# Expert weights in 2 MB pieces with 16 KB runs, activations turned in 32x32 blocks on VectorE

## The chip, the cores and the metric

The kernel runs on one core of one Trainium2 chip. The metric is the device time of one execution in microseconds (us). "Before" was run three times.

## What is computed

One encoder layer over 512 tokens of width 1024, all in float32: three token mixers with gates, then a mixture of 32 experts of which each token takes 4. The mixers are not touched by this change. The experts are:

```python
logits = ht @ w_router + b_router
top_v, top_i = lax.top_k(logits, 4);  gate = softmax(top_v)
# tokens are sorted by expert and worked on in blocks
def expert_block(xb, e):
    gu = xb @ w_gate_up[e] + b_gate_up[e]            # 1024 -> 2048
    g = minimum(gu[:, :1024], 7.0)
    lin = clip(gu[:, 1024:], -7.0, 7.0)
    act = g * sigmoid(1.702 * g) * (lin + 1.0)
    return act @ w_down[e] + b_down[e]               # 1024 -> 1024
y = segment_sum(rows * gate)                         # back to the tokens
x = rmsnorm(x + y, norm_final)
```

## The kernel before, in words

The program is written engine by engine, with semaphores between them; nothing reorders it. Each engine runs its own list, and a wait holds up everything behind it on that engine.

The mixers and the router fill the first part. Then comes the expert loop. A **job** is one expert with up to 96 token rows ("slots"); with these inputs there are 32 jobs, numbered 0 to 31. Per job, TensorE runs `gate_up(j)` and `down(j)`, and it works one job ahead: `gate_up(0)`, then in the loop `gate_up(j + 1)`, `down(j)`, and at the end `down_last(31)`.

- `gate_up` has 8 **parts**, one for each 128 rows of the contraction. Each part uses 1 MB of weights (`gu_w`), and runs 12 matmuls of 128x32 by 128x512 (24 records in the trace, since a float32 matmul leaves two). Ahead of the parts stand three small matmuls that write the bias (`bias_row` times `bias_of`).
- `down` has 4 parts of 1 MB (`dn_w`) with 24 matmuls of 128x32 by 128x256 each (48 records).
- The 96 rows of a job are fetched by an indirect DMA of GpSimd (`xg`), turned by TensorE with eight transposes against the identity (`turn_tokens`, at line 1434, after the first part of `down`) and copied by ScalarE into `xt`.
- After `gate_up`, ScalarE and VectorE make the activation: `sigmoid`, `clamp`, `activate`, which writes `act_sb` at line 1323. TensorE turns it with six transposes (`turn_act`) after part 1 of the next `gate_up`, and VectorE copies the result out of PSUM into `act_t` (`take_act`, line 1311), which `down` uses.
- After `down`, VectorE multiplies by the gate into `y_sb` (line 1331), and GpSimd adds the rows to `x_rows` in DRAM by three indirect DMAs.

Weights are loaded by the queue of SyncE (SP), in the order of its list. `gu_w` has two sets of eight buffers, `dn_w` one set of four. In the loop SP waits until a part of TensorE is done (`wait_part`, on the semaphore `gemm_ps`) and then issues the load into the buffer that it freed. A piece of `gu_w` or `dn_w` is one DMA of 128 partitions with 8 KB each. In the list the eight loads for `gate_up(j + 3)` stand behind the last `dn` load of `down(j)`, so they are issued in one go at the end of `down(j)`.

In job 0, between two parts of `gate_up`, TensorE also makes the tables of slots (`slot_tables`); the loop's first fetches of rows, and SP's loads of the last two pieces for job 1, wait for them. At the end, SP loads `final_gain` and `down_bias`, which `down_last`'s accumulation needs first.

Of the kernel before, what the change touches and what calls it, by code (L numbers as in the profile page):

```python
# [10 lines left out]
F32 = mybir.dt.float32  # L11
# [97 lines left out]
def encoder_kernel(nc, x, mem, norm_mix, w_in, q_norm_a, k_norm_a, sink_b, norm_mem, w_mem_kv,  # L109
# [3 lines left out]
    with ctx:  # L113
# [149 lines left out]
        gu_w = [sb(f"gu_w{i}", [P, 2 * D], F32, at * KIB) for i, at in enumerate(GU_AT)]  # L263
        dn_w = [sb(f"dn_w{i}", [P, 2 * D], F32, at * KIB) for i, at in enumerate(DN_AT)]
# [72 lines left out]
        gu_in = [sem(f"gu_in{i}") for i in range(16)]  # L337
        dn_in = [sem(f"dn_in{i}") for i in range(4)]
# [100 lines left out]
        at_ps = sem("at_ps")  # L439
# [115 lines left out]
        def _(sp):  # L555
# [44 lines left out]
            def load_gu(e, s, k):  # L600
                sp.dma_start(gu_w[s * KD + k][:], wgu[e, :, k, :]).then_inc(gu_in[s * KD + k], 16)  # L601

            def load_dn(e, q):
                sp.dma_start(dn_w[q][:], wdn[e, q, :, :]).then_inc(dn_in[q], 16)
# [17 lines left out]
            for k in (6, 7):
                load_gu(0, 0, k)
            for q in (0, 1):
                load_dn(0, q)
# [8 lines left out]
            for q in (2, 3):  # L634
                load_dn(0, q)
# [1254 lines left out]
```

## Time and profile before

| what | value |
|---|---|
| median of 3 runs | 1553.23 us (1552.82 to 1557.38) |
| the profiled execution | 1558.09 us, span 1556.2 us |
| TensorE (PE) busy | 1515.6 us, 97% |
| VectorE (DVE), ScalarE (ACT), GpSimd (POOL) busy | 27%, 19%, 15% |
| HBM read | 457.94 MB, 307 GB/s over the span |
| the weight loads | 256 of `gu_w` and 128 of `dn_w`, 1 MB each |

How to read the rows below. In a **timeline**, a row is the start in the span, the length, engine and line, the operation with "output <- input" and shape, the number of instructions merged into the row, and in brackets how long the engine had been idle before and what ended that. PE is the matmul side of TensorE; SPq and POOL issue DMAs. In a row of **windows**: stretch, its length, the busy time of PE, PEld (weight loads), DVE, ACT and POOL (number of instructions), granted clock of TensorE (1.00 is 2.4 GHz, 0.50 is 1.2 GHz), the mean share of the 16 DMA engines, GB/s. In rows of **DMA issues**: count, size of one, median us from issue to landing. [...]

### The profile page before, as it was taken

To read this page: it belongs to the slowest core of one execution; us is meant where nothing else is said; L and a number is where in the kernel's file an instruction comes from. 1 tells how busy PE (TensorE), PEld (TensorE's weight loads), DVE (VectorE), ACT (ScalarE), POOL (GpSimd) and SP (SyncE) were. 2 spreads that over 40 slices of the span, in tenths; PEclk is the share of its full clock that TensorE was granted. 3 is DMA by queue.
4 is the path that set the end of the run, shared out by engine and by line. 5 is a ranking of instruction groups with operands and counts; after the bars stand their busy time and mean duration, and the time that the engine had idled before them with its cause. 6 is when DMAs were issued, how large, how long until landed. Compare 5 with 4: busy or idle time off the path is not lost.

```text
span 1556.2 us, 35152 instructions
## 1 busy us (share of the span) xinstructions
PE 1515.6 (97%) x15156; PEld 780.8 (50%) x15156; DVE 423.5 (27%) x642; ACT 291.0 (19%) x519; POOL 225.8 (15%) x321
## 2 busy tenths in 40 slices
PE   8999999999989999999999999999999999999987
PEld 7866688888843343344333344433344443334432
DVE  3758722525532111121111121111121111112112
ACT  5468822323201000010000010000010000010001
POOL 0000030000010221111221111221111221111120
PEclk9999999999989999999999999999999999999998
DMA  7310022334768999999999999999999999999963
GB/s 266 120 67 22 8 91 75 123 140 186 289 254 299 388 387 384 396 387 401 396 387 390 387 398 395 391 388 386 386 395 393 385 379 383 384 384 395 407 226 126
DMA packets 98139, 468.75 MB, mean 301 GB/s; under 512 B 18360, under 2 KB 26832, under 8 KB 48912
## 3 DMA queue, kind: packets, MB, share of 16 engines
q1 hardware_dynamic: 79712, 450.35, 74.0%
q0 software_dynamic: 18048, 17.71, 5.6%
q8 instruction: 31, 0.51, 0.1%
q10 hardware_dynamic: 336, 0.08, 0.0%
q14 instruction: 12, 0.10, 0.0%
HBM read 457.94 MB, written 19.79 MB: 307 GB/s over the span
## 4 chain that ended last, share of the span: by engine, by line
PE 91%; DVE 3%; DMA 3%; SPq 1%; issue 1%; ACT 0%; ACTq 0%; DVEq 0%
PE ps L1755 41%; PE ps L1770 20%; PE ps L1407 6%; PE ps L1409 6%; PE ps L1408 6%; PE ps L1434 5%; DMA gu_w<-in_w_gate_up 2%; PE ps L1785 1%; PE ps L1560 1%; SPq L601 1%; DVE head_max L1086 1%; PE ps L1747 1%; PE ps L1516 1%; DVE probs L1104 1%; PE ps L1678 1%
## 5 line engine op out<-in xcount | busy, mean ns | idle before, releaser
L1755 PE MATMUL ps<-gu_w,xt 128*32 128x512 f32 x6144 | 675.6, 595 | 0.7 <-DMA gu_w<-in_w_gate_up 0.7
L1755 PEld LDWEIGHTS ps<-gu_w,xt 128*32 128x32 f32 x6144 | 192.9, 110 | 438.7 <-issue 434.3
L1770 PE MATMUL ps<-dn_w,act_t 128*32 128x256 f32 x5952 | 333.4, 380 | 0.1
L1770 PEld LDWEIGHTS ps<-dn_w,act_t 128*32 128x32 f32 x5952 | 189.7, 110 | 140.8 <-issue 15.4
L864 ACT ACTIVATE sg_sb<-ps,limits 128x768 f32<-128x768 f32 x32 | 28.9, 902 | 902.4 <-PE ps L1755 902.4
L1315 DVE TENSOR_SCALAR lin_sb<-ps 128x768 f32<-128x768 f32 x32 | 30.7, 958 | 493.0 <-ACT sg_sb L864 493.0
L949 POOL DMA_INDIRECT x_rows<-y_sb,sum_row x93 | 144.8, 1557 | 37.3 <-issue 37.3
L933 POOL TENSOR_TENSOR mark_sb<-ones 1x1 f32<-1x1 f32 x93 | 29.7, 319 | 796.9 <-DVE y_sb L1331 780.8
L1407 PE MATMUL ps<-w_high,h_hi 128*128 128x512 f32 x352 | 138.2, 392 | 0.6 <-DVE mem_lo L1032 0.5
L1409 PE MATMUL ps<-w_high,h_lo 128*128 128x512 f32 x352 | 137.1, 389 | 0.0
L1408 PE MATMUL ps<-w_low,h_hi 128*128 128x512 f32 x352 | 137.0, 389 | 0.0
L512 DVE TENSOR_TENSOR w_low<-w_raw,w_high 128x2048 fp32r<-128x2048 f32 (+2 forms) x36 | 63.9, 1813 | 116.1 <-ACT w_high L504 116.1
L1331 DVE TENSOR_TENSOR y_sb<-ps,y_gate 128x768 f32<-128x768 f32 x31 | 29.7, 957 | 206.6 <-PE ps L1770 206.6
L1311 DVE COPY act_t<-ps 128x768 f32<-128x768 f32 x32 | 30.6, 958 | 174.6 <-PE ps L1434 167.9
L1407 PEld LDWEIGHTS ps<-w_high,h_hi 128*128 128x128 f32 x352 | 66.1, 188 | 15.0 <-DVE mem_lo L1032 0.8
L1409 PEld LDWEIGHTS ps<-w_high,h_lo 128*128 128x128 f32 x352 | 66.1, 188 | 13.8
L1408 PEld LDWEIGHTS ps<-w_low,h_hi 128*128 128x128 f32 x352 | 66.1, 188 | 13.2
L504 ACT ACTIVATE w_high<-w_raw 128x2048 fp32r<-128x2048 f32 (+2 forms) x36 | 53.5, 1537 | 19.5 <-PE ps L1409 17.6
L1323 DVE SCALAR_TENSOR_TENSOR act_sb<-lin_sb,sg_sb 128x768 f32<-128x768 f32 x32 | 50.7, 1584 | 3.3
L756 ACT ACTIVATE probs<-ps,neg_max 128x512 f32<-128x512 f32 (+2 forms) x64 | 37.5, 595 | 5.5 <-DVE neg_max L1089 5.2
L943 POOL DMA_INDIRECT xg<-h_rows,gather_row x32 | 33.0, 1033 | 26.1 <-issue 20.0
L860 ACT ACTIVATE xt<-ps 128x768 f32<-128x768 f32 x32 | 25.9, 811 | 56.5 <-PE ps L1434 56.5
(255 smaller groups left out, 1006.0 us busy)
## 6 DMA issues: line engine op xcount, KB each, us to landing
gu_w<-in_w_gate_up SPq DMA_DIRECT2D x256, 1024.0 KB, 25.3
dn_w<-in_w_down SPq DMA_DIRECT2D x128, 1024.0 KB, 18.7
w_raw<-in_w_in SPq DMA_DIRECT2D x8, 2048.0 KB, 7.9
w_raw<-in_w_out SPq DMA_DIRECT2D x2, 2048.0 KB, 7.7
w_raw<-in_w_in SPq DMA_DIRECT2D x2, 1024.0 KB, 7.5
x_sb<-in_x SPq DMA_DIRECT2D x8, 256.0 KB, 7.0
w_raw<-in_w_mem_kv SPq DMA_DIRECT2D x1, 2048.0 KB, 10.1
x<-in_x SPq DMA_DIRECT2D x4, 512.0 KB, 5.0
```

Source lines behind the costliest of these rows:

```text
L504: nc.scalar.activation(wh[u % 2][:, a * COLS:b * COLS], raw[u % 2][:, a * COLS:b * COLS], ACT.Copy).then_inc(wh_done, 1)
L512: nc.vector.tensor_tensor(wl[u % 2][:, a * COLS:b * COLS], raw[u % 2][:, a * COLS:b * COLS], wh[u % 2][:, a * COLS:b * COLS].bitcast(F32), ...
L756: nc.scalar.activation(probs[:, 2 * (s % 2) + g, 0:w], ps[:, 2 * (s % 2) + g, 0:w], ACT.Exp, bias=neg_max[:, s % 2, g:g + 1], scale=SCALE, ...
L943: nc.gpsimd.indirect_dma_start(out=xg[s][:], out_offset=None, in_=h2_rows, in_offset=bass.IndirectOffsetOnAxis(ap=rows, axis=0), bounds_ch ...
L949: nc.gpsimd.indirect_dma_start(out=x_rows.rearrange("r (q n) -> (r q) n", q=4), out_offset=bass.IndirectOffsetOnAxis(ap=sum_row[:, s, g:g ...
L1323: nc.vector.scalar_tensor_tensor(out=act_sb[:].rearrange("p (h g) c -> p (g c) h", h=2), in0=lin_sb[:].rearrange("p g (c h) -> p (g c) h", ...
L1407: nc.tensor.matmul(bank, hi, w_hi, start=start, stop=False)
L1408: nc.tensor.matmul(bank, hi, w_lo, start=False, stop=False)
L1409: return nc.tensor.matmul(bank, lo, w_hi, start=False, stop=stop)
L1434: return nc.tensor.transpose(ps[0:src.shape[1], bank, col:col + n], src, ident[0:n, 0:n])
L1755: last = nc.tensor.matmul(ps[quarter(q), g, :], xt[:, k, quarter(g)], w[:].rearrange("p (h n) -> p h n", h=2)[:, :, q * QCOLS:(q + 1) * QC ...
L1770: last = nc.tensor.matmul(ps[quarter(q), 3 + g, 0:QCOLS], act_t[:, TRIOS * h + g, quarter(c)], dn_w[c][:, h * D + q * QCOLS:h * D + (q + 1 ...
```

## The change

1. The weights are laid out differently. `gate_up`'s contraction row on partition p of part c is now row 8p + c, in place of 128c + p, and likewise for `down`. One DMA loads two parts: 128 partitions with 16 KB of consecutive rows each, 2 MB. Semaphores and SP's waits go by pairs.
2. To match, `turn_tokens` picks every eighth column of `xg`, and `activate` writes `act_sb` in blocks of 32 columns.
3. The six transposes of TensorE for the activation are gone, and the copy out of PSUM with them. VectorE does one `transpose` (32x32 blocks, SBUF to SBUF) in `turn_act`, after `take_y`. ScalarE waits for `act_ready` before it overwrites `sg_sb`.
4. `bias_of` is loaded and cast at the program's start, by ScalarE's queue and GpSimd, in place of SP and VectorE ahead of the expert loop.
5. `slot_tables` run after part 2 of `gate_up(0)`, in place of part 4.
6. `final_gain` and `down_bias` are loaded ahead of the last `dn` loads.

```diff
-        gu_w = [sb(f"gu_w{i}", [P, 2 * D], F32, at * KIB) for i, at in enumerate(GU_AT)]
-        dn_w = [sb(f"dn_w{i}", [P, 2 * D], F32, at * KIB) for i, at in enumerate(DN_AT)]
+        gu_pair = [sb(f"gu_pair{i}", [P, 4 * D], F32, at * KIB) for i, at in enumerate(GU_AT[0::2])]
+        dn_pair = [sb(f"dn_pair{i}", [P, 4 * D], F32, at * KIB) for i, at in enumerate(DN_AT[0::2])]
+        gu_w = [gu_pair[i // 2][:, (i % 2) * 2 * D:(i % 2 + 1) * 2 * D] for i in range(16)]
+        dn_w = [dn_pair[i // 2][:, (i % 2) * 2 * D:(i % 2 + 1) * 2 * D] for i in range(4)]
...
-        wgu = w_gate_up[0].rearrange("e (k p) n -> e p k n", p=P)
-        wdn = w_down[0].rearrange("e (q p h) n -> e q p (h n)", p=P, h=2)
+        wgu = w_gate_up[0].rearrange("e (p k a) n -> e k p (a n)", p=P, a=2)
+        wdn = w_down[0].rearrange("e (p q h) n -> e q p (h n)", p=P, h=4)
...
             sp.wait_ge(gate_t_ps, 1)
-            for k in range(KD - 2, KD):
-                load_gu(e_one, 1, k)
+            load_gu(e_one, 1, GU_PAIRS - 1)
...
-                    for k in range(KD):
-                        wait_part(sp, i, b * PARTS + k)
-                        if k == 0:
+                    for m in range(GU_PAIRS):
+                        wait_part(sp, i, b * PARTS + 2 * m + 1)
+                        if m == 0:
                             load_bias(e_gu, b)
-                        load_gu(e_gu, b, k)
-                    for q in range(DN_PARTS):
-                        wait_part(sp, i, stream(b, KD + q))
-                        load_dn(e_dn, q)
+                        load_gu(e_gu, b, m)
+                    for m in range(DN_PAIRS):
+                        wait_part(sp, i, stream(b, KD + 2 * m + 1))
+                        load_dn(e_dn, m)
             e_last = sp.value_load(job_table[0:1, 0, bass.ds(pairs_but_one * 2 + 1, 1)], min_val=0, max_val=N_EXP - 1)
-            for q in range(DN_PARTS):
-                wait_part(sp, pairs_but_one, stream(0, KD + q))
-                load_dn(e_last, q)
-
-
             wait_part(sp, pairs_but_one, stream(0, KD - 1))
             sp.dma_start(final_gain[:], norm_final.rearrange("(a n) -> a n", a=1).to_broadcast([P, D])).then_inc(fgain_in, 16)
             for t in range(TB):
                 sp.dma_start(down_bias[N_EXP * t:N_EXP * (t + 1), :], b_down[0]).then_inc(down_bias_in, 16)
+            for m in range(DN_PAIRS):
+                wait_part(sp, pairs_but_one, stream(0, KD + 2 * m + 1))
+                load_dn(e_last, m)
...
+            act.dma_start(bias_of_raw[:], fixed[:, 5 * P + 8:6 * P + 8]).then_inc(bias_of_in, 16)
...
+                    act.wait_ge(act_ready, j + 1)
                     sigmoid(j + 1)
...
+            pool.wait_ge(bias_of_in, 16)
+            nc.gpsimd.tensor_copy(bias_of[:], bias_of_raw[:]).then_inc(bias_of_ready, 1)
...
-            def take_act(j):
-                dve.wait_ge(at_ps, j + 1)
-                nc.vector.tensor_copy(act_t[:].rearrange("p (a k) m -> p a (k m)", a=2), ps[:, 6:8, 0:TRIOS * P]).then_inc(act_t_done, 1)
+            def turn_act(j):
+                dve.wait_ge(act_ready, j + 1)
+                nc.vector.transpose(act_t[:], act_sb[:]).then_inc(act_t_done, 1)
...
-                nc.vector.scalar_tensor_tensor(out=act_sb[:].rearrange("p (h g) c -> p (g c) h", h=2), in0=lin_sb[:].rearrange("p g (c h) -> p (g c) h", h=2),
-                                               scalar=1.0, in1=sg_sb[:].rearrange("p g (c h) -> p (g c) h", h=2),
+                nc.vector.scalar_tensor_tensor(out=act_sb[:].rearrange("p (c x) -> p x c", c=KD), in0=lin_sb[:].rearrange("p g (i c) -> p (g i) c", c=KD),
+                                               scalar=1.0, in1=sg_sb[:].rearrange("p g (i c) -> p (g i) c", c=KD),
...
-            dve.wait_ge(bias_of_in, 16)
-            nc.vector.tensor_copy(bias_of[:], bias_of_raw[:]).then_inc(bias_of_ready, 1)
...
-                    take_act(j)
                     wait_part(dve, i, stream(b, KD - 1))
                     clamp(j + 1)
+                    dve.wait_ge(act_t_done, j + 1)
                     activate(j + 1)
                     wait_part(dve, i, stream(b, PARTS - 1))
                     take_y(j, b)
-            take_act(pairs_but_one * 2)
+                    turn_act(j + 1)
...
             wait_part(dve, pairs_but_one, stream(0, PARTS - 1))
-            take_act(pairs_but_one * 2 + 1)
+            turn_act(pairs_but_one * 2 + 1)
             take_y(pairs_but_one * 2, 0)
...
-                if k == 4:
+                if k == 2:
                     pe.wait_ge(vals_ready, 1)
...
             def turn_tokens(s):
                 for k in range(KD):
-                    last = turn(6 + k // 4, (k % 4) * SLOTS, xg[s][:, k * P:(k + 1) * P])
+                    last = turn(6 + k // 4, (k % 4) * SLOTS, xg[s][:].rearrange("s (p k) -> s k p", k=KD)[:, k, :])
                 last.then_inc(x_ps, 1)
-
-            def turn_act(j):
-                pe.wait_ge(act_ready, j + 1)
-                for k in range(2 * TRIOS):
-                    last = turn(6 + k // TRIOS, (k % TRIOS) * P, act_sb[:, k, :])
...
+
+            def act_part(k, g):
+
+                return act_t[:, k * SLOTS + QUARTER * g:k * SLOTS + QUARTER * (g + 1)]
...
                 for k in range(KD):
                     w = gu_w[s * KD + k]
-                    pe.wait_ge(gu_in[s * KD + k], loads * 16)
+                    if k % 2 == 0:
+                        pe.wait_ge(gu_in[s * GU_PAIRS + k // 2], loads * 16)
...
                 for c in range(DN_PARTS):
-                    pe.wait_ge(dn_in[c], j * 16 + 16)
+                    if c % 2 == 0:
+                        pe.wait_ge(dn_in[c // 2], j * 16 + 16)
                     for h in range(2):
                         for g in range(TRIOS):
                             for q in range(4):
-                                last = nc.tensor.matmul(ps[quarter(q), 3 + g, 0:QCOLS], act_t[:, TRIOS * h + g, quarter(c)],
+                                last = nc.tensor.matmul(ps[quarter(q), 3 + g, 0:QCOLS], act_part(2 * c + h, g),
...
             pe.wait_ge(gs_ready, j + 1)
             pe.wait_ge(l_ready, j + 1)
-            gate_up(j + 1, 1, pairs_but_one + 1, last_act_but_one)
-            down(j, last_act_of_all)
+            gate_up(j + 1, 1, pairs_but_one + 1, lambda k: None)
+            down(j, lambda q: None)
```

How the lists change, at three places. On TensorE, in the loop, around the second part of `gate_up` (each buffer of before serves one part, each pair of after two). Before:

```order
L1755 MATMUL ps<-gu_w_158,xt 32x512 x11
L1755 MATMUL ps<-gu_w_159,xt 32x512 [waits gu_in1]
L1755 MATMUL ps<-gu_w_159,xt 32x512 x11
L1434 MATMUL ps<-ident,act_sb 128x128 [waits act_ready]
L1434 MATMUL ps<-ident,act_sb 128x128 x5
L1755 MATMUL ps<-gu_w_160,xt 32x512 [waits gu_in2]
```

And now:

```order
L1753 MATMUL ps<-gu_pair_158,xt 32x512 [waits gu_in0]
L1753 MATMUL ps<-gu_pair_158,xt 32x512 x23
L1753 MATMUL ps<-gu_pair_159,xt 32x512 [waits gu_in1]
L1753 MATMUL ps<-gu_pair_159,xt 32x512 x23
L1753 MATMUL ps<-gu_pair_160,xt 32x512 [waits gu_in2]
```

The turns of `act_sb` are gone, and only every other part waits for a load. On VectorE, one job of the loop (`under_limit`, `sg_ready` come from ScalarE, `gemm_ps` from TensorE, `added` from GpSimd's scatter). Before:

```order
L1311 COPY act_t<-ps 128x768 [waits at_ps]
L550 ISA
L1314 REGISTER_ALU [waits gemm_ps]
L1315 TENSOR_SCALAR lin_sb<-ps 128x768 [waits under_limit]
L1319 SCALAR_TENSOR_TENSOR sg_sb<-ps,sg_sb 128x768 [waits sg_ready]
L1323 SCALAR_TENSOR_TENSOR act_sb<-lin_sb,sg_sb 128x384x2 [waits gs_ready,l_ready]
L550 REGISTER_ALU
L1330 ISA [waits gate_kept,gemm_ps]
L1331 TENSOR_TENSOR y_sb<-ps,y_gate 128x768 [waits added]
```

And now:

```order
L1313 ISA [waits gemm_ps]
L1314 TENSOR_SCALAR lin_sb<-ps 128x768 [waits under_limit]
L1350 REGISTER_ALU
L1318 SCALAR_TENSOR_TENSOR sg_sb<-ps,sg_sb 128x768 [waits sg_ready,act_t_done]
L1322 SCALAR_TENSOR_TENSOR act_sb<-lin_sb,sg_sb 128x96x8 [waits gs_ready,l_ready]
L553 REGISTER_ALU
L1329 ISA [waits gate_kept,gemm_ps]
L1330 TENSOR_TENSOR y_sb<-ps,y_gate 128x768 [waits added]
L1310 STREAM_TRANSPOSE act_t<-act_sb 128x768 [waits act_ready]
```

The copy at the job's start is replaced by a transpose at its end, behind `y_sb`. On SP, after the loop, the loads for the last job. Before:

```order
L604 ISA [waits gemm_ps]
L604 DMA dn_w_176<-in_w_down 128x2048
L550 REGISTER_ALU
L604 ISA [waits gemm_ps]
L604 DMA dn_w_177<-in_w_down 128x2048
L550 REGISTER_ALU
L666 DMA final_gain<-in_norm_final 128x1024 [waits gemm_ps]
L668 DMA down_bias<-in_b_down 32x1024 x4
```

And now:

```order
L553 ISA
L657 DMA final_gain<-in_norm_final 128x1024 [waits gemm_ps]
L659 DMA down_bias<-in_b_down 32x1024 x4
L553 REGISTER_ALU
L607 ISA [waits gemm_ps]
L607 DMA dn_pair_166<-in_w_down 128x4096
L553 REGISTER_ALU
L607 ISA [waits gemm_ps]
L607 DMA dn_pair_167<-in_w_down 128x4096
```

`final_gain` and the four loads of `down_bias` stand ahead of the two `dn` loads, which wait for two parts each.

## Rows read from the trace of the kernel before

**Rows 1.** The head of the profile's page.
```profile
span 1556.2 us, 35152 instructions
```

**Rows 2.** Windows: the loop, the start of the experts, and `down_last`.
```profile
900.00:1000.00 100.00, 100.00 (x1205) 40.95 (x1199) 15.99 (x16) 8.02 (x11) 19.48 (x27) 1.00 1.02 391
...
441.00:446.00 5.00, 5.00 (x27) 1.19 (x28) 0.00 (x0) 0.00 (x0) 1.05 (x1) 0.50 1.02 433
...
1524.00:1528.00 4.00, 4.00 (x17) 0.96 (x18) 0.00 (x0) 0.00 (x0) 0.00 (x0) 0.50 1.01 401
```

**Rows 3.** Timeline of TensorE over one job of the loop.
```profile
1007.54 5.36 PE L1755 MATMUL ps<-gu_w,xt 128*32 128x512 f32 x48
1012.83 0.87 PE L1434 MATMUL ps<-ident,act_sb 128*128 128x128 f32 x6
1013.63 15.66 PE L1755 MATMUL ps<-gu_w,xt 128*32 128x512 f32 x144
...
1031.81 0.88 PE L1434 MATMUL ps<-ident,xg 96*128 96x96 f32 x8
```

**Rows 4.** Timeline of VectorE: `y_sb` of two neighbouring jobs, and of two four apart.
```profile
1241.28 0.96 DVE L1331 TENSOR_TENSOR y_sb<-ps,y_gate 128x768 f32<-128x768 f32 x1 [6.85 <-PE ps L1770]
...
1274.70 0.96 DVE L1331 TENSOR_TENSOR y_sb<-ps,y_gate 128x768 f32<-128x768 f32 x1 [6.86 <-PE ps L1770]
...
1308.24 0.96 DVE L1331 TENSOR_TENSOR y_sb<-ps,y_gate 128x768 f32<-128x768 f32 x1 [6.99 <-PE ps L1770]
...
1444.10 0.96 DVE L1331 TENSOR_TENSOR y_sb<-ps,y_gate 128x768 f32<-128x768 f32 x1 [7.09 <-PE ps L1770]
```

**Rows 5.** DMA issues of `dn_w`, from 500 to 600 and from 1300 to 1400.
```profile
dn_w<-in_w_down SPq DMA_DIRECT2D x12, 1024.0 KB, 7.2
...
dn_w<-in_w_down SPq DMA_DIRECT2D x12, 1024.0 KB, 29.9
```

**Rows 6.** The page's groups: VectorE's copy out of PSUM and its strided product.
```profile
L1311 DVE COPY act_t<-ps 128x768 f32<-128x768 f32 x32 | 30.6, 958 | 174.6 <-PE ps L1434 167.9
...
L1323 DVE SCALAR_TENSOR_TENSOR act_sb<-lin_sb,sg_sb 128x768 f32<-128x768 f32 x32 | 50.7, 1584 | 3.3
```

**Rows 7.** Timeline from the first job to the first `dn` load of the loop.
```profile
440.38 1.66 POOL L972 TENSOR_TENSOR job_vals<-job_hots,dest_vals 128x880 f32<-128x880 f32 x1
...
440.49 0.80 PE L1747 MATMUL ps<-bias_row,bias_of 8*128 8x512 f32 x3 [5.80 <-issue]
441.22 15.65 PE L1755 MATMUL ps<-gu_w,xt 128*32 128x512 f32 x120
...
472.38 0.51 PE L1747 MATMUL ps<-bias_row,bias_of 8*128 8x512 f32 x3 [1.04 <-DVE sg_sb L1319]
...
497.36 6.46 SPq L604 DMA_DIRECT2D dn_w<-in_w_down  x3
```

**Rows 8.** DMA, 10 to 17 (2 KB packets) and 437 to 450 (8 KB).
```profile
DMA packets 1422, 2.75 MB, mean 393 GB/s; under 512 B 80, under 2 KB 80, under 8 KB 1422
...
q1 hardware_dynamic: 1422, 2.75, 105.3%
...
DMA packets 716, 5.27 MB, mean 405 GB/s; under 512 B 73, under 2 KB 73, under 8 KB 73
...
q1 hardware_dynamic: 716, 5.27, 97.1%
```

**Rows 9.** Timeline of the end: last part of `down(30)` to `down_last`'s result.
```profile
1507.98 2.80 PE L1770 MATMUL ps<-dn_w,act_t 128*32 128x256 f32 x48
...
1520.45 3.78 PE L1837 MATMUL ps<-down_bias,gate_t 32*128 32x512 f32 x8 [9.67 <-DMA down_bias<-in_b_down]
...
1524.16 16.05 PE L1785 MATMUL ps<-dn_w,act_t 128*32 128x512 f32 x96
1540.28 1.26 ACT L895 ACTIVATE y_hi_last<-ps,last_gate 96x512 fp32r<-96x512 f32 x2 [37.26 <-PE ps L1785]
```

More of the change, by code:

```diff
@@ L271, in encoder_kernel @@
         xg = [sb(f"xg{i}", [SLOTS, D], F32, (166 + 4 * i) * KIB) for i in range(2)]
-        act_t = sb("act_t", [P, 2 * TRIOS, P], F32, 174 * KIB)
+        act_t = sb("act_t", [P, KD * SLOTS], F32, 174 * KIB)
         lin_sb = sb("lin_sb", [P, TRIOS, QCOLS], F32, 177 * KIB)
         sg_sb = sb("sg_sb", [P, TRIOS, QCOLS], F32, 180 * KIB)
-        act_sb = sb("act_sb", [P, 2 * TRIOS, P], F32, 184 * KIB)
+        act_sb = sb("act_sb", [P, KD * SLOTS], F32, 184 * KIB)
         same_slot = sb("same_slot", [SLOTS, TRIOS, P], F32, 196 * KIB)
@@ L336, in encoder_kernel @@
         first_in = sem("first_in")
-        gu_in = [sem(f"gu_in{i}") for i in range(16)]
-        dn_in = [sem(f"dn_in{i}") for i in range(4)]
+        gu_in = [sem(f"gu_in{i}") for i in range(8)]
+        dn_in = [sem(f"dn_in{i}") for i in range(2)]
         bias_of_in = sem("bias_of_in")
@@ L598, in _, with load_gu, load_dn @@
                 sp.dma_start(x2[:, t, :], x[0, t * P:(t + 1) * P, :]).then_inc(x2_in, 16)
[L600 to L604, printed above, removed]
+            def load_gu(e, s, m):
+                sp.dma_start(gu_pair[s * GU_PAIRS + m][:], wgu[e, m, :, :]).then_inc(gu_in[s * GU_PAIRS + m], 16)
+            def load_dn(e, m):
+                sp.dma_start(dn_pair[m][:], wdn[e, m, :, :]).then_inc(dn_in[m], 16)
             def load_bias(e, s):
@@ L610, in _ @@
             sp.wait_ge(bias_stored, 256)
-            sp.dma_start(bias_of_raw[:], fixed[:, 5 * P + 8:6 * P + 8]).then_inc(bias_of_in, 16)
             load_bias(0, 0)
-            for k in (0, 1):
-                load_gu(0, 0, k)
+            load_gu(0, 0, 0)
             for n in range(2):
                 sp.wait_ge(wl_done, 2 * (UNITS - 1 + n))
-                for k in (2 + 2 * n, 3 + 2 * n):
-                    load_gu(0, 0, k)
+                load_gu(0, 0, 1 + n)
             sp.dma_start(h2_rows[SEQ:SEQ + SLOTS, :], x[0, 0:SLOTS, :]).then_inc(rows_out, 16)
             sp.wait_ge(gemm_ps, GEMMS[UNITS - 1])
[L622 to L625, printed above, removed]
+            load_gu(0, 0, 3)
+            load_dn(0, 0)
             for t in range(TB):
@@ L633, in _ @@
             sp.wait_ge(gemm_ps, G1)
-            for q in (2, 3):
-                load_dn(0, q)
+            load_dn(0, 1)
             sp.wait_ge(table_ready, 1)
@@ L639, in _ @@
             load_bias(e_one, 1)
-            for k in range(KD - 2):
-                load_gu(e_one, 1, k)
+            for m in range(GU_PAIRS - 1):
+                load_gu(e_one, 1, m)
             sp.wait_ge(vals_ready, 1)
             sp.wait_ge(gate_t_ps, 1)
-            for k in range(KD - 2, KD):
-                load_gu(e_one, 1, k)
+            load_gu(e_one, 1, GU_PAIRS - 1)
             pairs_but_one = sp.value_load(job_table[0:1, 1, 1:2], min_val=MIN_PAIRS - 1, max_val=NJ // 2 - 1)
@@ L888, in _ @@
             wait_part(act, pairs_but_one, stream(0, KD - 1))
+            act.wait_ge(act_ready, pairs_but_one * 2 + 1)
             sigmoid(pairs_but_one * 2 + 1)
@@ L1344, in _ @@
             activate(0)
+            turn_act(0)
             take_sum_rows()
@@ L1720, in turn_tokens @@
                 for k in range(KD):
-                    last = turn(6 + k // 4, (k % 4) * SLOTS, xg[s][:, k * P:(k + 1) * P])
+                    last = turn(6 + k // 4, (k % 4) * SLOTS, xg[s][:].rearrange("s (p k) -> s k p", k=KD)[:, k, :])
                 last.then_inc(x_ps, 1)
-            def turn_act(j):
-                pe.wait_ge(act_ready, j + 1)
-                for k in range(2 * TRIOS):
-                    last = turn(6 + k // TRIOS, (k % TRIOS) * P, act_sb[:, k, :])
-                last.then_inc(at_ps, 1)
             def spread_slots():
@@ L1780, in down_last @@
                 for c in range(DN_PARTS):
-                    pe.wait_ge(dn_in[c], j * 16 + 16)
+                    if c % 2 == 0:
+                        pe.wait_ge(dn_in[c // 2], j * 16 + 16)
                     for h in range(2):
@@ L1784, in down_last @@
                             for g in range(TRIOS):
-                                last = nc.tensor.matmul(ps[quarter(g), 4 + n, :], act_t[:, TRIOS * h + g, quarter(c)],
+                                last = nc.tensor.matmul(ps[quarter(g), 4 + n, :], act_part(2 * c + h, g),
                                                         dn_w[c][:, h * D + n * COLS:h * D + (n + 1) * COLS],
@@ L1813, in _ @@
                     pe.wait_ge(l_ready, j + 1)
-                    gate_up(j + 1, 1 - b, i + 1 + b, last_act)
+                    gate_up(j + 1, 1 - b, i + 1 + b, lambda k: None)
                     if b == 0:
```

17 lines of the change are left out of this document (5 added, 12 removed).

## Prediction

> Times are span microseconds unless said otherwise. The profiled execution took 1558.1 us, its span is 1556.2 [rows 1], and the median of the runs shown is 1553.2. I work in the span and carry the difference over to the median.
>
> **What bounds the kernel now.** I read the windows first. In the expert loop TensorE is busy without a gap at full clock, and the DMA engines show a share of 1.02 beside it [rows 2]. So two things are full at once, and the question is which one sets the pace. The timeline of TensorE gives what a job consists of: gate_up, in its middle the six turns of act_sb, then down with eight turns of xg after its first part [rows 3]. The 144 records after the act turns take 15.66 us and the 48 before them 5.36, so a record costs 10.30/96 = 0.107 us. 48 of them end 5.15 us after 1007.54, at 1012.69, and the next gate_up record starts at 1013.63: the act turns cost the path **0.94 us** a job.
>
> The starts of y_sb, one a job, are 33.42 us apart (1241.28 to 1274.70), and four jobs later on average 33.97 (135.86/4) [rows 4]. The times to landing say why: a piece of dn_w landed 7.2 us after its issue around 550 and 29.9 around 1350 [rows 5]. A piece is issued when its buffer is read and needed one job, 33.4 us, later. The queue was slower than TensorE all along; it ate the slack and at about 1300 TensorE began to wait a little. So: **PE pace 33.42, queue's own pace 33.97** (12 pieces of 1 MB a job), and the kernel ends as the slack is gone. A change that only frees TensorE meets the queue. That is the core of the case.
>
> **The change, part by part.**
>
> *Act turns leave TensorE.* 33.42 - 0.94 = 32.48 a job. VectorE does a 32x32 block transpose of 128x768 instead of the copy out of PSUM. The trace has no such operation: the nearest rows are the copy, 958 ns, and the strided product, 1584 ns [rows 6]; I take 1.3 us. In the loop it runs after y_sb and is wanted a whole gate_up later, over 20 us, so it costs nothing there. Without that cover it would cost its 1.3 us; it has none once, in front of down_last. The product's new write pattern (eight elements in place of two inside) and ScalarE's new wait on act_ready, met a job earlier, are hidden in down too.
>
> *The start.* TensorE stood 5.80 us in front of its first bias matmul at 440.49, whose operand bias_of VectorE casts late. GpSimd does that at the program's start now, so gate_up(0) can start once xt is there, near 435.7 in place of 441.22: 5.5 us. Its first 120 records took 15.65 us [rows 7], partly at the lower of the two clock levels, 1.2 GHz (0.50 granted, 441 to 446, after that idle time [rows 2]); at 0.107 us they take 12.9. That is 2.8 more. The slot tables move from part 4 to part 2: reached at 435.7 + 7.7 = 443.4, while GpSimd's last product for them ended at 442.04 [rows 7], so no wait, but with 1.4 us to spare only. gate_up(1) begins at 472.38 - 8.3 = **464.1**. The tables' turn also releases the fourth pair of gu(1) some 13 us earlier, so the queue doesn't run dry at 455; it still does ahead of down(0).
>
> *Pairs of 2 MB.* dn(1) is what the queue waits for at the start: issued at 497.36, 24.98 after gate_up(1) began [rows 7]. Now it needs two parts of down(0) and the xg turns (2.6 + 0.9) but no act turns (0.9): 464.1 + 27.5 = **491.6**. After that the queue is never empty. A pair needs both its parts free and both landed, up to 5 us less slack out of 26; once the queue sets the pace this costs only the time of the last pair's two parts, 5.2 us.
>
> *16 KB runs.* Price per packet by two stretches [rows 8]: 1342 packets of 2 KB (without 80 small ones) in 105.3% of 7 us x 16 engines, at most 88 ns each; 643 of 8 KB (without 73) in 97.1% of 13 x 16, 314 ns. Four of 2 KB cost 351, so each packet has some 12 ns of its own; two of 8 KB joined save 12 of 628, 1.9%. Of 33.97 that is at most 0.6; the scatter and gather share the queue and keep theirs. I take 0.47: **pace 33.5**. Bounds: 33.97 (nothing saved) above, and below 33.2, under which TensorE is the limit again. The rows are now 64 KB apart (dn: 32 KB) in place of end to end. The 2 KB packets of w_raw came from rows 18 KB apart and lost nothing but their own 12 ns, so I put no price on that; the other side is a rival. The Trainium skill (DMA: Bandwidth & Descriptors, Latency and other measured facts) reports falling rates with row pitch from 2 MiB up and the full rate at 512 KiB. By that rule nothing is lost here; this trace has no such pitch.
>
> *Strided xg.* The eight turns of xg now load every eighth element. Their time is unchanged in my sum; see the rivals.
>
> *The end.* Down(30) ends at 1507.98 + 2.80 = 1510.8. Then TensorE stood 9.67 us for down_bias, issued behind the last dn piece, ran the bias matmuls for 3.78 us and down_last for 16.05, its first 4 us at granted clock 0.50 [rows 2, 9]. Now final_gain and down_bias are issued at the end of gate_up(31), 11 us ahead. Counted from the end of down(30): transpose 1.3, y_sb 1.0 = 2.3; bias matmuls 2.0 at full clock; down_last 13.9; the rest as before, 1556.2 - 1540.28 = 15.9. Sum **34.1** for 45.4. What is late next: dn(31)'s pairs. In queue order they land some 3.4 and 9.1 us after down(30)'s end (1 MB of gains and biases, then 2 MB at 5.7 each); down_last wants them at 4.3 and 11. It fits, closely.
>
> **The sum.** Two chains; the later one ends down(30).
> - TensorE: 464.1 + 31 x 32.48 = 1471.0, less 0.9, since down(30) has no turns left at all: 1470.1. (The same for before: 472.38 + 31 x 33.42 = 1508.4, and 2.4 of waits, 1510.8.)
> - Queue: dn(1) to dn(30) and gu(3) to gu(31), 352 MB or 29.33 jobs: 491.6 + 29.33 x 33.5 = 1474.2, and 5.2 for the last two parts: **1479.4**. (Before: 497.4 + 29.33 x 33.97 = 1493.7.)
>
> 1479.4 + 34.1 = 1513.5, that is 42.7 less than 1556.2; median 1553.2 - 42.7 = **1510.5**, said as 1511. 11.3 of it come from the end, 31.4 from what lies before (8.3 of these from TensorE's start). The queue takes back some 8 us of what TensorE could have had.
>
> **Rivals.**
> 1. *Nothing saved by longer runs.* Pace 33.97: queue 1488.0, down(30) 1493.2, median 1524. For it: the 12 ns come from different stretches. Chance 0.14.
> 2. *TensorE remains the limit.* Pace under 33.2: 1470.1 + 34.1, median 1501. It can't be beaten without a TensorE gain that I see nowhere. 0.13.
> 3. *Strided xg is dear.* No row loads weights with a stride. A turn of xg spaces out at 0.88/8 = 0.11 us [rows 3]; if each doubled, the job is back to nearly 33.4, down(30) ends at 464.1 + 31 x 33.4 = 1499.5, median 1531. Against it: the loads run beside the matmuls. The Trainium skill (SBUF — State Buffer, Door 1) says that an access needs two hits in a 16-byte line for full rate; a 32-byte step has one. By that rule this rival holds; no row shows it. 0.10.
> 4. *Slower, the other side: scattered runs.* If reads 64 KB apart slow the queue, median = 1510.5 + 29.33 x (pace - 33.5). From a pace of 34.96, 2.9% over today's, the kernel is slower than before; at 5% over, 35.7, it is 1575. For it: all the loop's bytes come so, and nothing else can absorb it. Against: the 18 KB rows. 0.10.
> 5. *The end keeps a wait* (dn(31) late): up to 11 back, 1522. 0.05.
>
> My forecast, pace 33.2 to 33.9, has 0.48 and by itself spans 1501 to 1522.
>
> **Numbers.** About 0.3% (5 us) is what a measurement of this kernel tells from no change. The range must hold the forecast, rivals 1, 2, 3 and 5: 1500 to 1533. Faster 0.88 (all but rival 4 and some sum of misfortunes), same 0.03, slower 0.09.
>
> **What would show it.** Right: y_sb starts 32.5 us apart at first and about 33.5 later; waits of TensorE on dn_pair and gu_pair, growing from the middle on; 16 KB packets near 616 ns, one engine's time; no idle of 5.8 at 435 and none of 9.7 after down(30); clock 1.00 at both places. Wrong: 33.4 from the first job on with no DMA wait (rival 3), a pace over 34 with full queue (rival 4), a stall at the slot tables, or down_last waiting for dn_in.

## Result, and the profile after

The changed kernel takes 1540.7 us (median of four, 1538.3 to 1542.1), the kernel before beside it 1555.3 (four, 1552.8 to 1557.8). The ratio is 0.9904, 95% interval 0.9879 to 0.9929: faster by 1%, where I had forecast nearly 3%; the measured time lies outside my range. The profiled execution took 1541.8 us. Of the run e14 below, two of six executions took 2567 and 2967 us and are left out of its time; what disturbed them is not known.

First VectorE's timeline after the change: `y_sb` of the first two jobs, and of two jobs thirteen apart (compare [rows 4]).

```profile
499.89 0.96 DVE L1330 TENSOR_TENSOR y_sb<-ps,y_gate 128x768 f32<-128x768 f32 x1 [6.99 <-PE ps L1769]
532.62 0.96 DVE L1330 TENSOR_TENSOR y_sb<-ps,y_gate 128x768 f32<-128x768 f32 x1 [7.07 <-PE ps L1769]
...
990.88 0.96 DVE L1330 TENSOR_TENSOR y_sb<-ps,y_gate 128x768 f32<-128x768 f32 x1 [7.14 <-PE ps L1769]
...
1439.44 0.96 DVE L1330 TENSOR_TENSOR y_sb<-ps,y_gate 128x768 f32<-128x768 f32 x1 [9.00 <-PE ps L1769]
```

A job takes 32.73 us at first, and does so for fifteen jobs. From 990.88 on it takes (1439.44 - 990.88)/13 = 34.50 us. That is slower than any job of the kernel before. Windows say the same: span 1539.9, and between 1300 and 1400 TensorE is no longer full (columns as in [rows 2]; why a DMA share can pass 1.00, as in [rows 8] for one queue alone, no run here shows).

```profile
900.00:1000.00 100.00, 99.79 (x1205) 40.67 (x1201) 15.94 (x15) 8.22 (x12) 20.37 (x31) 1.00 1.02 394
1300.00:1400.00 100.00, 96.05 (x1121) 37.16 (x1117) 16.07 (x15) 8.22 (x12) 19.50 (x27) 1.00 1.01 384
```

The waits of TensorE over the whole span (us in total, times, longest): the late jobs wait for the second matrix.

```profile
PE ps L1769 <- DMA dn_pair<-in_w_down: 15.2, 25, 1.3
...
PE ps L1744 <- DVE sg_sb L1318: 2.6, 1, 2.6
...
PE ps L1753 <- DMA gu_pair<-in_w_gate_up: 0.6, 3, 0.2
```

The loads between 500 and 600, then between 1300 and 1400 (compare [rows 5]):

```profile
gu_pair<-in_w_gate_up SPq DMA_DIRECT2D x12, 2048.0 KB, 20.1
dn_pair<-in_w_down SPq DMA_DIRECT2D x7, 2048.0 KB, 9.9
...
gu_pair<-in_w_gate_up SPq DMA_DIRECT2D x12, 2048.0 KB, 37.5
dn_pair<-in_w_down SPq DMA_DIRECT2D x6, 2048.0 KB, 28.3
```

The start (compare [rows 7]) and the end ([rows 9]):

```profile
464.26 0.80 PE L1744 MATMUL ps<-bias_row,bias_of 8*128 8x512 f32 x3 [2.60 <-DVE sg_sb L1318]
464.98 23.19 PE L1753 MATMUL ps<-gu_pair,xt 128*32 128x512 f32 x192
...
494.75 5.51 SPq L607 DMA_DIRECT2D dn_pair<-in_w_down  x2
...
1503.95 0.98 DVE L1310 STREAM_TRANSPOSE act_t<-act_sb 128x768 f32<-128x768 f32 x1 [5.80 <-PE ps L1769]
1504.85 0.92 DVE L1330 TENSOR_TENSOR y_sb<-ps,y_gate 128x768 f32<-128x768 f32 x1
1505.92 2.28 PE L1825 MATMUL ps<-down_bias,gate_t 32*128 32x512 f32 x8 [2.04 <-DVE y_sb L1330]
...
1508.13 15.29 PE L1785 MATMUL ps<-dn_pair,act_t 128*32 128x512 f32 x96
```

gate_up(1) starts at 464.26. The wait of 9.67 us ahead of down_bias is gone. Down(30) ends at 1503.9: 6.9 us earlier than before, where I had expected 31.4.

**A view of my own.** The semaphore of a load is raised 16 times, and the trace has the times. The page counts 16 DMA engines, and I read each signal as that of one engine; the trace does not name them. For one `dn` load, in us after the first of the 16:

```
kernel, issued at   the sixteen engines in order of landing
before,  1301.0     0 .1 .1 .1 .1 .2 .7 .7 1.1 1.3 1.4 3.5 5.6 10.9 14.5 21.7
after,    560.2     0 .2 .3 .9 1.0 1.2 1.4 1.4 1.6 1.7 1.7 2.0 2.2 2.3 2.5 2.5
after,    920.2     0 .1 .1 .8 1.5 2.9 6.1 7.1 8.6 8.7 11.3 11.9 12.4 13.8 15.9 16.3
after,   1301.0     0 .3 .4 .4 .4 .8 1.0 1.1 1.7 2.6 7.9 11.0 11.4 15.0 17.8 22.0
```

So "the queue" is not one thing. In both kernels some engines fall behind, job by job, until the last is about 22 us late, while ten or eleven of the sixteen land within 3 us of each other at 1301. TensorE may start only after the last of the 16 signals. The landing time of [rows 5] is that of the laggards. Below, "lag" is the last number of such a row.

### The profile page after: what moved, and what is told of

It is laid out like the page before. It is cut to its first block, busy times and chain, and to the rows that moved or that the text cites. A ratio compares the mean times of both kernels' runs of the same rounds, so it can differ in the third digit from the quotient of the medians.

```text
span 1539.9 us, 34114 instructions
## 1 busy us (share of the span) xinstructions
PE 1496.6 (97%) x14964; PEld 768.7 (50%) x14964; DVE 420.0 (27%) x641; ACT 290.9 (19%) x519; POOL 226.3 (15%) x322
## 3 DMA queue, kind: packets, MB, share of 16 engines
q0 software_dynamic: 18048, 17.71, 5.5%
## 4 chain that ended last, share of the span: by engine, by line
PE 71%; DMA 25%; DVE 3%; ACT 1%; issue 0%; ACTq 0%; SPq 0%; DVEq 0%
PE ps L1753 26%; DMA dn_pair<-in_w_down 24%; PE ps L1769 17%; PE ps L1406 6%; PE ps L1408 6%; PE ps L1407 6%; PE ps L1433 3%; PE ps L1785 1%; PE ps L1559 1%; DVE head_max L1085 1%; PE ps L1515 1%; DVE probs L1103 1%; PE ps L1677 1%; PE ps L1744 1%; PE ps L1442 0%
## 5 line engine op out<-in xcount | busy, mean ns | idle before, releaser
L1753 PE MATMUL ps<-gu_pair,xt 128*32 128x512 f32 x6144 | 670.2, 595 | 1.2 <-DMA gu_pair<-in_w_gate_up 0.6
L1753 PEld LDWEIGHTS ps<-gu_pair,xt 128*32 128x32 f32 x6144 | 195.3, 110 | 454.4 <-issue 431.1
L1769 PE MATMUL ps<-dn_pair,act_t 128*32 128x256 f32 x5952 | 336.2, 380 | 15.3 <-DMA dn_pair<-in_w_down 15.2
L1769 PEld LDWEIGHTS ps<-dn_pair,act_t 128*32 128x32 f32 x5952 | 187.6, 110 | 162.3 <-DMA dn_pair<-in_w_down 34.9
L1407 PEld LDWEIGHTS ps<-w_low,h_hi 128*128 128x128 f32 x352 | 66.1, 188 | 13.3
L505 ACT ACTIVATE w_high<-w_raw 128x2048 fp32r<-128x2048 f32 (+2 forms) x36 | 53.5, 1538 | 19.5 <-PE ps L1408 17.6
L1433 PEld LDWEIGHTS ps<-ident,xg 96*128 96x128 f32 x256 | 30.9, 204 | 13.2 <-issue 12.3
```

What stands on the lines that cost most here:

```text
L505: nc.scalar.activation(wh[u % 2][:, a * COLS:b * COLS], raw[u % 2][:, a * COLS:b * COLS], ACT.Copy).then_inc(wh_done, 1)
L1407: nc.tensor.matmul(bank, hi, w_lo, start=False, stop=False)
L1433: return nc.tensor.transpose(ps[0:src.shape[1], bank, col:col + n], src, ident[0:n, 0:n])
L1753: last = nc.tensor.matmul(ps[quarter(q), g, :], xt[:, k, quarter(g)], w.rearrange("p (h n) -> p h n", h=2)[:, :, q * QCOLS:(q + 1) * QCOLS ...
L1769: last = nc.tensor.matmul(ps[quarter(q), 3 + g, 0:QCOLS], act_part(2 * c + h, g), dn_w[c][:, h * D + q * QCOLS:h * D + (q + 1) * QCOLS], s ...
```

## Experiments

The question was why some engines lag. The page counts GpSimd's gathers and scatters (queue q0 below) on the same 16 engines. Their rows are valid only up to the count of an expert's tokens (40 to 96 of 96 slots, 64 on average) and the rest is skipped. Places are filled from slot 0 up, so the work lies on the first partitions.

**e1, slots spread.** Where a place's slot is chosen, the two comparisons get another order of the same numbers:

```diff
-tensor_tensor(slot_hot[:], counter[:, 0:SLOTS].rearrange("p (a j) -> p a j", a=1) ...
+tensor_tensor(slot_hot[:].rearrange("p c (x b) -> p c x b", b=4),
+              counter[:, 0:SLOTS].rearrange("p (a b x) -> p a x b", a=1, b=4) ...
```

> The changed kernel, with consecutive places of an expert's tokens put on slots four apart (slot 4x+b holds place 24b+x), so that the rows which gathers and scatters really move lie on all partitions and not on the first ones of each block; the output stays the reference's. Theory 1 (the slowest DMA engines set the pace, and they are slow because the scatter and gather rows fall on few engines): the spread between the first and the last engine's landing of a load falls from about 20 us to under 8 us, TensorE's jobs in the second half take 33.0 to 33.3 us and not 34.5, and the time is 1518 to 1527 us. Theory 2 (the engines lag for another reason: long runs, or a fixed difference of the engines): spread and pace stay, 1538 to 1543 us.

Measured: **1518.9 us**, ratio 0.9767 (0.9754 to 0.9781). Every job takes 32.73 us:

```profile
501.14 0.96 DVE L1332 TENSOR_TENSOR y_sb<-ps,y_gate 128x768 f32<-128x768 f32 x1 [6.99 <-PE ps L1771]
...
1417.49 0.96 DVE L1332 TENSOR_TENSOR y_sb<-ps,y_gate 128x768 f32<-128x768 f32 x1 [7.00 <-PE ps L1771]
```

That is 916.35/28 = 32.73. Packets and bytes are the same in both kernels. Queue q0 is that of the gathers and scatters, over the whole span (packets, MB, share of 16 engines):

```profile
q1 hardware_dynamic: 51920, 450.27, 74.4%
q0 software_dynamic: 18048, 17.71, 5.5%
```

Only the place of the rows differs. The lag is 6.9 at 921 us and 13.3 at 1314, and stays under 16; in the changed kernel TensorE's waits came at about 20. Theory 1 holds in its cause and its time. Two of its sizes were off: the lag is not under 8, and the late jobs take 32.73 us, not 33.0 to 33.3.

**e2, the start and the end alone.** The kernel before, with:

```diff
-            sp.dma_start(bias_of_raw[:], ...)       # on SP, cast by VectorE late
+            act.dma_start(bias_of_raw[:], ...)      # on ACT, cast by GpSimd early
-                if k == 4:                          # slot_tables
+                if k == 2:
-            for q in range(DN_PARTS): ... load_dn(e_last, q)
             sp.dma_start(final_gain[:], ...)
             for t in range(TB): sp.dma_start(down_bias[...], ...)
+            for q in range(DN_PARTS): ... load_dn(e_last, q)
```

> The kernel before with only what the change did outside the loop: bias_of made early, the slot tables at block 2 of gate_up(0), the last down loads behind the final gain and bias. The loop (1 MB pieces, turns on TensorE) stays. Theory 1 (in the loop both kernels go at the pace of the slowest DMA engines, so the change of the loop bought next to nothing; start 3 to 6 us and end 9 to 10 us are the whole gain): 1539 to 1543 us, as the changed kernel. Theory 2 (the loop change gave about half): 1546 to 1551 us.

Measured: **1540.2 us**, 0.9905 (0.9888 to 0.9922), the changed kernel's time. The whole change of the loop bought nothing that I can measure here.

**e3, loads of 1 MB,** the changed kernel with runs of 8 KB:

```diff
-wgu = w_gate_up[0].rearrange("e (p k a) n -> e k p (a n)", p=P, a=2)
+wgu = w_gate_up[0].rearrange("e (p k) n -> e k p n", p=P)
-wdn = w_down[0].rearrange("e (p q h) n -> e q p (h n)", p=P, h=4)
+wdn = w_down[0].rearrange("e (p q h) n -> e q p (h n)", p=P, h=2)
```

> The changed kernel with loads of 1 MB and runs of 8 KB (rows 8p+c and the block transposes stay). Theory 1 (the length of a run does not matter where the slowest engine sets the pace): 1538 to 1543 us. Theory 2 (16 KB runs save 0.47 us a job as I summed it): 29 jobs by 0.47 is 14 us more, 1550 to 1556 us. Theory 3 (2 MB pieces come free later, two blocks at once, and that costs the queue its lead): less, 1525 to 1535 us.

Measured: **1539.9 us**, 0.9898 (0.9883 to 0.9913). Run length and piece size changed together, and their sum does not show in the time. It shows in the lag: 17.7 us at 827 us in e3, 12.5 in the changed kernel, at the same 32.73 us a job. So long runs may have helped the late engines, and the larger pieces may have taken it back; no run here parts the two.

**e4, e3 with the old rows,** its turns of xg unstrided:

```diff
-wgu = ... "e (p k) n -> e k p n"            wdn = ... "e (p q h) n -> e q p (h n)"
+wgu = ... "e (k p) n -> e k p n"            wdn = ... "e (q p h) n -> e q p (h n)"
-xg[s][:].rearrange("s (p k) -> s k p", k=KD)[:, k, :]
+xg[s][:, k * P:(k + 1) * P]
```

> The 1 MB kernel of the run above, and the weights' rows taken as before (128 neighbouring rows of w_gate_up a piece, 256 of w_down, each piece one stretch of memory), with the unstrided turns of xg; the rows of w_down then do not match the order of the activations, so what it computes is another sum. Theory 1 (scattered runs cost nothing, strided turns 0.24 us a job only where TensorE is the limit): within 2 us of the 1 MB kernel in the queue-bound half, 16 early jobs at 32.45 us and not 32.72, so at most 4 us less. Theory 2 (scattered runs, 32 or 64 KB apart, keep the queue at 34.5 us): 8 to 16 us less.

Measured: **1538.6 us**, 0.9895 (0.988 to 0.991). Jobs of 32.48 us up to some 860 us, then 34.3. The faster TensorE only meets the laggards sooner.

**e5, e2 with the slots spread.**

> The kernel before with the new start and end and with the spread slots (turns on TensorE, 1 MB pieces). Theory 1 (its TensorE needs 33.42 us a job, and the slowest engine keeps that pace once the rows are spread; so the slots alone save only the few late jobs of 33.8 to 34.2 us): 1.5 to 3 us less than the run with the ends alone, 1537 to 1539 us, every job 33.4. Then the loop change is worth 18 to 20 us where the slots are spread and nothing where they are not. Theory 2 (the spread slots are the whole gain, whatever the loop does): 1519 to 1525 us.

Measured: **1539.2 us**, 0.9898 (0.9882 to 0.9913), 33.42 us a job to the end, and a lag under 10. Theory 1, but the slots alone save 1.0 us beside e2, not 1.5 to 3. The loop's change is worth 1539.2 - 1518.9 = 20.3 us once the slots are spread, and nothing before.

**e6, e1 with unstrided turns.** Only w_down keeps rows 8p+c:

```diff
-wgu = ... "e (p k a) n -> e k p (a n)", a=2      # 16 KB runs
+wgu = ... "e (k a p) n -> e k p a n", a=2        # two 8 KB runs
```

> The changed kernel with spread slots, and w_gate_up in its old rows (a load of 2 MB with two runs of 8 KB on each partition) and the turns of xg unstrided; only w_down keeps rows 8p+c, which the block transposes need. Output the reference's. Theory 1 (strided turns cost TensorE 0.24 us a job, and TensorE is the limit with spread slots): 32.48 us a job, 29 by 0.24 is 7 us less than with the slots alone, 1511 to 1514 us. Theory 2 (the slowest engine, some 33.2 us a job there, takes over before the end): 1515 to 1519 us, with the late jobs over 33 us.

Measured: **1520.5 us**, 0.9773 (0.9756 to 0.9789). 32.48 us a job for 22 jobs, then 33.5 to 35.1 with a lag of 20. Neither theory had the size: the late jobs cost as much as the early ones saved.

**e7 and e8, what fills the laggards.** Each is the changed kernel with one kind of row skipped:

```diff
-    compute_op=ALU.add, bounds_check=4 * SEQ - 1      # e7, the scatters
+    compute_op=ALU.add, bounds_check=0
-    gather(..., bounds_check=SEQ - 1)                 # e8, the gathers in the loop
+    gather(..., bounds_check=0)
```

> The changed kernel (slots not spread), whose scatters skip every row but row 0, so the weighted sums are left out and 1 KB packets all but vanish. Theory S (the scatters' rows are what slows some engines): the spread of a load's landings stays under 8 us, all jobs 32.7 us, 1516 to 1522 us. Theory G (the gathers' 4 KB rows are): spread near 20 us, 1536 to 1541 us. Theory B (bias_row, on eight partitions, is): the same, 1538 to 1541 us.

> The changed kernel (slots not spread), whose gathers in the loop skip every row but row 0, so the jobs work on tokens of the first gathers; scatters move as before. Theory S: spread near 20 us, 1536 to 1541 us. Theory G: spread under 8 us and 1516 to 1522 us. Both in part: each of the two runs lies at 1525 to 1535 us, with the jobs slower than 32.7 us only from a later job on.

Measured: **1517.45 us** (0.9756, 0.9741 to 0.9771), and **1519.08 us** (0.9762, 0.9746 to 0.9777); a lag of 2.9 at 1316 us and of 0.7 at 1314, never over 3.5 in either. I had expected one or the other, or a half from each. Leaving out either one cures all of it: beside the weights the late engines keep up with one kind of row, and only both together are too much for them.

**e9, weights' rows 256m+2p+a** (16 KB runs, 2 MB in one stretch, xg read every second element), slots as in e1.

> The changed kernel with spread slots (4x+b) and w_gate_up in rows 256m+2p+a: a load of 2 MB is then one stretch of memory with 16 KB a partition, and the turns of xg read every second element (8 bytes apart) and not every eighth (32 bytes). Output the reference's. Theory 1 (a step of 8 bytes costs TensorE little, but at 32.5 us a job the slowest engine takes over late, as in the run with unstrided turns): 32.5 us a job up to some 22nd job and 33.5 to 34.5 after it, 1517 to 1521 us. Theory 2 (the late slow jobs of that run came from its 8 KB runs or their two places): all jobs 32.5, 1511 to 1514 us.

Measured: **1517.65 us**, 0.9758 (0.9737 to 0.9778). The time lies in theory 1's range, but by luck: no late job is slow, and both theories fell. TensorE takes 32.80 us a job: a step of 8 bytes is no cheaper than one of 32. The groups of the weight loads for the eight turns between 500 and 1400 us, first in the changed kernel, then in e6, then in e9:

```profile
L1433 PEld LDWEIGHTS ps<-ident,xg 96*128 96x128 f32 x216 | 26.1, 204 | 11.1 <-issue 11.1
```
```profile
L1435 PEld LDWEIGHTS ps<-ident,xg 96*128 96x128 f32 x216 | 18.8, 140 | 11.1 <-issue 11.1
```
```profile
L1435 PEld LDWEIGHTS ps<-ident,xg 96*128 96x128 f32 x216 | 28.0, 217 | 11.1 <-issue 11.1
```

**e10 and e11, spread "more finely"** (e1 and e9 with b=8: slot 8x+b holds place 12b+x).

> The changed kernel with the slots spread more finely: slot 8x+b holds place 12b+x, so that each eight neighbouring slots hold the same number of rows within one, where 4x+b left up to six of eight in the first third of them. Theory 1 (evenness of rows over the engines is what counts): the spread of a load's landings at the end is under 10 us and not 15, all jobs 32.7 us, 1517 to 1520 us as with 4x+b, since TensorE is the limit there. Theory 2 (what is left of the lag has another source): the spread at the end stays 13 to 16 us.

> Both edits of the two runs above. Theory 1 (finer spreading gives the queue the room that a faster TensorE needs): all jobs 32.5 us, 1511 to 1514 us, the best version. Theory 2 (the slowest engine takes over late in any case): 1515 to 1520 us.

Measured: **1541.3 us** (0.991, 0.989 to 0.993) and **1539.2 us** (0.9894, 0.9875 to 0.9912). My idea of evenness was wrong. The engines of e10, at 821.0:

```
0 0 0 .1 .3 .4 .5 .5 3.6 5.9 8.8 9.5 11.5 11.9 14.5 16.5
```

Eight engines keep up to within half a us and eight lag. With slot 8x+b, b from 5 to 7 is nearly empty. That fits an engine chosen by b's highest bit, worth four partitions: groups of four neighbouring partitions to an engine, at least for one of the two kinds of row. I took it as the rule for both.

**e12, a slot order made for groups of four** (places 0 to 31 on slots 32 to 63, the others dealt over the groups of 0 to 31 and 64 to 95), and **e13**, the same with e6's rows.

> The changed kernel with the first 32 places of a block on slots 32 to 63, and the other 64 dealt one by one to the sixteen groups of four slots in 0 to 31 and 64 to 95. Output the reference's. Theory M (rows go to the engine whose number is that of the group of four partitions, modulo 16; a gather's 96 rows then give engines 0 to 7 two groups and 8 to 15 one): by the experts' token counts and the packets' times (186 ns a gathered row, 101 ns a scattered quarter) the most loaded engine had 0.74 us a job more than the mean without spreading, 0.38 with 4x+b, 1.53 with 8x+b, and has 0.15 here. So the landings of a load spread by less than 6 us at 1300 us (13 with 4x+b), all jobs take 32.7 us, 1517 to 1520 us. Rival (the engine goes by other bits of the partition, with which the central third is not special): 0.5 us or more above the mean, spread 12 us or more there.

> The same slots, with w_gate_up in its old rows and the turns of xg unstrided, as in the run e6_gu_plain_spread, whose TensorE went at 32.48 us a job until the slowest engine was a set of weights behind, and then at 34. Theory M: the lag grows too slowly to matter, all jobs 32.5 us, 1510 to 1514 us. Rival (at 32.5 us a job all engines together are at their limit, 30.9 us of weights and 2.4 us of rows a job): late jobs over 33 us again, 1515 to 1521 us.

Measured: **1527.0 us** (0.9815, 0.9798 to 0.9832), lag 19.4 at 1317; and **1530.9 us** (0.9843, 0.9827 to 0.986). Both lie outside what I had said, and the rule fell in this form. I then fitted: for each way of choosing an engine from a row's number, the lag of all 16 engines at 921 us in e1, e10, e12 and the changed kernel, with one threshold for all. Best of some 1,500 combinations, each with four pairs of costs for the two kinds of row: a gather's 96 rows go **six neighbours to an engine**, a scatter's 128 **four neighbours to an engine, then round again after 64**. The time that fits a gathered row is 0.3 us, not its packet's 0.19. The scatter's half of the rule is not settled by it: the four quarters of a slot's row lie 32 partitions apart, and with partitions p and p + 32 on one engine and those from 64 up on the other eight, every engine gets the same sum in every one of these orders. It is a fit, so it was put to an order that it had not seen.

**e14, slot 6x+b holds place 16b+x** (e1's edit with b=6), the flattest of the simple orders by that rule, and **e15**, the same with e6's rows and turns.

> The changed kernel with slot 6x+b holding place 16b+x. Output the reference's. Theory F (fitted: a gather's rows go six neighbours to an engine, a scatter's by groups of four modulo 16): the landings of a load spread by 5 us at 921 us (6.9 measured with 4x+b, 16.3 without spreading, 20.4 with 8x+b) and by 7 to 10 us at 1314 us (13.3 with 4x+b); all jobs 32.7 us, 1517 to 1520 us. Rival (the fit to four orders is luck): spread at 921 us of 7 us or more.

> The same slots with w_gate_up in its old rows and the turns of xg unstrided (TensorE 32.48 us a job). Theory F: the lag grows by 0.25 us a job more than in the run before, to 14 or 15 us at the end, short of the 20 at which jobs slow down: all jobs 32.5 us, 1511 to 1514 us. Rival (at this pace all engines together are at their limit): late jobs over 33 us, 1516 to 1524 us, as with the other two slot orders.

Measured: e14 a lag of **5.3** at 917 and **7.9** at 1310, all jobs 32.73, ratio 0.9771 (0.9755 to 0.9786), 1519.3 us by the median of four executions. e15: **1511.95 us**, 0.9717 (0.9702 to 0.9731), all jobs 32.48, lag 10.2 at 1306. It is the fastest version, 2.8% under the kernel before, and computes the same. That its time is that of my forecast is chance: every job runs at TensorE's pace. Its landing times between 1300 and 1400 us, beside 37.5 and 28.3 above:

```profile
gu_pair<-in_w_gate_up SPq DMA_DIRECT2D x12, 2048.0 KB, 30.4
dn_pair<-in_w_down SPq DMA_DIRECT2D x6, 2048.0 KB, 20.3
```

## Why the prediction was wrong

**The step that failed** is "the queue was slower than TensorE all along ... queue's own pace 33.97", and with it the pace of 33.5 after. I took the queue as one server with one pace, read from the late jobs. It was right that the slack was eaten and that TensorE then waits. But 33.97 was no pace of the queue: with the rows spread it delivers the same 12 MB in every 32.48 us (e15). A few engines ate the slack. They fall behind at a rate that is TensorE's pace against theirs: at 33.42 us a job (e2) the lag is 11.5 at 926 us, at 32.73 (after) 16.3, and the slow jobs begin near 1370 and 990. With the slots as they were, down(30) ends when those engines are done, whatever TensorE does: the last `y_sb` starts at 1504.0 in e2, 1504.8 after, 1505.6 in e3, 1502.3 in e4, with TensorE's own paces of 33.42, 32.73, 32.73 and 32.48. (In e2 the two limits meet: e5, with TensorE's pace of 33.42 to the end, has it at 1503.8.) Thirteen jobs at 34.50 in place of 32.73 are 23.0 us; e1, where they take 32.73, has its last `y_sb` at 1482.5, 22.3 earlier than the changed kernel. That is nearly all of the 24.5 by which down(30) is later than my 1479.4, though my 1479.4 came from a queue at 33.5 and not from this.

My own sum for the kernel before showed the fault. The queue at 33.97 ends at 1493.7, and with the last part of 2.8 us down(30) would end near 1496.5 and TensorE's chain, 1508.4, would never wait. It ended at 1510.8 after waits. So the last engine stood more than 14 us behind the pace that I gave to all of them. (Also, 1479.4 is 9.3 us behind TensorE's 1470.1, not "some 8".)

**16 KB runs** were to save 0.47 us a job. In the time they saved nothing that shows: e3 equals the changed kernel. The price of the packets was nearly right: in the changed kernel a 16 KB packet takes 620 ns by its median from 500 to 700 and 625 from 1200 to 1400, two of 8 KB in e3 626 to 628, and in e15, which has both kinds, 615 and 628. What failed is that this small saving would set the pace. Rival 1 is what held for the time, but even its pace of 33.97 was 0.5 too low.

**Act turns off TensorE**, 0.94 us: exact. e4, e6 and e15, with unstrided turns of xg, go at 32.48 us a job. **The block transpose** takes 0.97 us, not 1.3, and hides as said; the product kept its 1.57.

**Strided xg** was set at nothing. It costs 32.73 - 32.48 = 0.25 us a job: its weight load takes 204 ns and not 140. The Trainium skill (SBUF — State Buffer, Door 1) spoke for such a cost, and rival 3 had the mechanism; the doubling that I priced, 0.88 us, was three and a half times too much. By that rule the step of 8 bytes in e9, which has two hits in 16 bytes, should have been free; it took 217 ns. For these weight loads the measurement goes against the rule, and what makes a strided one dearer is open.

**Scattered runs** (rival 4): nothing. e3 and e4 differ by 1.3 us. My sign for this rival, a pace over 34 with a full queue, did appear, but the late engines made it.

**The start**: gate_up(1) at 464.26 for 464.1. But the stretch at half clock only moved: it was 441 to 446 [rows 2], now the windows have 0.50 between 463 and 468, around the end of the idle time of 2.60, and gate_up(1) took 23.19 us, where its 192 records at 0.107 are 20.6. So dn(1) was issued at 494.75, 3.1 later than I said.

**The end**: 36.0 us from the end of down(30) for 34.1. The wait for down_bias is gone, as said, and dn(31) is in time. The bias matmuls and down_last took 17.6 and not 15.9, since here too half clock came back for some us:

```profile
463.00:468.00 5.00, 3.74 (x19) 1.09 (x23) 3.94 (x5) 0.83 (x2) 0.00 (x0) 0.50 0.99 423
...
1507.00:1511.00 4.00, 4.00 (x18) 0.84 (x17) 0.00 (x0) 0.00 (x0) 3.39 (x3) 0.57 0.98 399
```

**Open**: the late engines' own pace. TensorE's pace plus the growth of the lag a job should give it, and mostly does: from 560 to 958 us the changed kernel's lag grows by 1.25 to 1.44 us a job, which stands for 34.0 to 34.2, and its late jobs take 34.5; in e12 it stands for 33.7, and they take 33.5. But in e6 (some 17 us over 22 jobs at 32.48) it stands for 33.3, and the five late jobs take 34.3. Open too is what makes a gathered row cost more than its packet. The rule for engines is fitted to four orders and foretold a fifth; no row of a trace names an engine. That the order of the slots makes the lag, and that the lag makes the late jobs, is shown; which engine carries which row is not.

## What to carry to other kernels

A DMA share of 1.0 and a growing landing time don't give the pace of a queue: look at the 16 signals of one load first. Where half of them come early, ask what small transfers run beside the loads and how their rows lie in the partitions. Here they were 4% of the bytes. Freeing TensorE gained nothing until they were spread, and 20 us after. Before pricing an edit in the loop, ask which single engine ends last, and try the sum on the kernel before: it must give the time that you already have.

## What the hardware showed that I had not expected

- Where the rows of a gather or scatter lie in the partitions decides how late the last of a load's 16 signals comes. The same 18048 packets in another order of slots moved the kernel between 1541 (the changed kernel, and 8x+b) and 1519 us (4x+b and 6x+b).
- Leaving out either the gathers or the scatters took the lag near 1300 us from 22 us to 0.7 or 2.9: what counts is the sum of both on the latest engine.
- A weight load of 96x128 from a strided operand took 204 ns (every eighth element) or 217 (every second), from a dense one 140.
- A 32x32 block transpose of 128x768 took VectorE 969 ns, as long as its copy out of PSUM (958).
- Removing an idle time of 5.80 us did not remove the half-clock stretch beside it: it came at the next, shorter one (2.60 us). At the end an idle time of 2.04 us was followed by one in the changed kernel, and by none in e5, e6 and e9.
